# Hybrid gMLP and dilated-attention block on eight cores: V groups as separate keys, banks chosen by disuse, and a written-out order for the input part

## The reference

```
h = rms_norm(x, norm_mix_pre);  z = h @ w_in
u_a, v_a, q, k, v_b, g_a, g_b = split(z)
y_a = gelu(u_a) * (tril(w_s) @ layer_norm(gelu(v_a)) + b_s)   # in chunks of 128
y_b = mixture over (window, dilation) = (128,1), (512,4), (2048,16)
      of softmax attention with ALiBi, 16 heads of 64
merged = sigmoid(g_a + b0) * (y_a @ w_a_proj) + sigmoid(g_b + b1) * (y_b @ w_b_proj)
x = x + rms_norm(merged @ w_out, norm_mix_post)
out = x + rms_norm(square(relu(rms_norm(x, norm_ffn_pre) @ w_ff1)) @ w_ff2, norm_ffn_post)
```

## Time and profile before

| what | us |
|---|---|
| median of 3 runs (1236.28 to 1341.39) | 1237.54 |
| the profiled execution's own time | 1236.43 |
| its span, first to last instruction, core 6 | 1234.9 |
| spans of the 8 cores | 1231.5 to 1234.9 |
| first scores of pair 0 start | 59.99 |
| last V product of pair 7 | about 396 |

### The profile page before, as it was taken

How to read it: one execution, slowest core, us unless ns; L and a number is a source line. 1 busy time by engine, 2 the same in 40 slices (tenths; PEclk the granted TensorE clock), 3 DMA queues, 4 the chain that set the end, 5 groups by cost and what they waited for, 6 DMA issues and landing times.

```text
span 1234.9 us, 23134 instructions; the slowest of 8 cores (1231.5 to 1234.9 us)
## 1 busy us (share of the span) xinstructions
PE 1183.3 (96%) x8072; PEld 606.6 (49%) x8203; DVE 564.8 (46%) x971; ACT 544.3 (44%) x910; POOL 152.6 (12%) x207
## 2 busy tenths in 40 slices
PE   6899999999999999999999999999999999999997
PEld 3455655565566445544444444444444444444443
DVE  3656766676677867723223354400560046103303
ACT  4565776666687553221212464420552055204411
POOL 2100000000010547621100000000000101010100
PEclk8999999999999999999999999999999999999999
DMA  9521532431134579499972223625363536353741
GB/s 241 133 49 40 107 55 44 81 70 37 30 62 83 103 105 136 86 178 135 128 107 35 89 82 107 234 72 202 120 226 132 204 120 199 117 193 135 245 152 69
DMA packets 37106, 146.39 MB, mean 119 GB/s; under 512 B 5120, under 2 KB 5376, under 8 KB 28288
## 3 DMA queue, kind: packets, MB, share of 16 engines
q0 software_dynamic: 21504, 104.87, 37.4%
q1 hardware_dynamic: 15488, 40.03, 10.7%
HBM read 165.85 MB, written 25.17 MB: 155 GB/s over the span
## 4 chain that ended last, share of the span: by engine, by line
PE 87%; DVE 5%; issue 3%; ACT 2%; DMA 2%; DVEq 0%; SPq 0%; ACTq 0%; POOLq 0%
PE pss L259 36%; PE psc L259 27%; PE psa L259 21%; PE psa L353 2%; DVE sb_PT L519 2%; ACT sb_Et L498 1%; DMA sb_xt<-x 1%; DMA sb_wqkv<-w_qkv 1%; DVE sb_vaug L362 1%; DVE sb_VT L339 0%; DVE sb_bst L621 0%; DVE sb_ybT L568 0%; ACT sb_junk L288 0%; DVE sb_acc L559 0%; PE pss L304 0%
## 5 line engine op out<-in xcount | busy, mean ns | idle before, releaser
L498 ACT ACTIVATE sb_Et<-pss 128x1024 bf16<-128x1024 f32 x144 | 139.7, 1015 | 50.8 <-PE pss L259 34.8
L976 DVE TENSOR_TENSOR sb_hT<-sb_hT 128x512 bf16<-128x512 bf16 x128 | 50.8, 421 | 231.9 <-ACT sb_hT L974 231.9
L259 PE MATMUL psa<-sb_hT,sb_wqkv 128*128 128x512 bf16 x516 | 125.1, 382 | 12.7 <-DVE sb_vaug L362 3.8
L519 DVE TENSOR_TENSOR sb_PT<-sb_Et,sb_EBh 128x512 bf16<-128x512 bf16 x208 | 84.8, 422 | 24.8 <-ACT sb_Et L498 12.9
L764 ACT ACTIVATE sb_sg<-pss,sb_bg 128x512 f32<-128x512 f32 x50 | 34.4, 687 | 137.2 <-PE pss L259 126.3
L259 PE MATMUL pss<-sb_hT,sb_wg 128*128 128x512 bf16 x407 | 93.9, 379 | 0.5
L259 PE MATMUL pss<-sb_w2b,sb_hT 128*128 128x512 bf16 x283 | 84.6, 379 | 0.3
L777 DVE SCALAR_TENSOR_TENSOR sb_sg<-sb_sg,psc 128x512 f32<-128x512 f32 x50 | 34.4, 688 | 109.4 <-PE psc L259 109.4
L259 PEld LDWEIGHTS psa<-sb_hT,sb_wqkv 128*128 128x128 bf16 x552 | 49.3, 98 | 64.8 <-issue 14.3
L259 PE MATMUL pss<-sb_h2T,sb_w1b 128*128 128x512 bf16 x342 | 78.7, 379 | 0.5
L259 PE MATMUL psc<-sb_PT,sb_vaug 128*128 128x128 bf16 (+1 forms) x752 | 67.9, 232 | 0.4 <-DVE sb_PT L519 0.3
(11 more groups left out here) (201 smaller groups left out, 1938.9 us busy)
## 6 DMA issues: line engine op xcount, KB each, us to landing
sb_w1b<-w_bf POOLq DMA_DIRECT2D x23, 1024.0 KB, 6.9
sb_mgw<-w_bf POOLq DMA_DIRECT2D x21, 1024.0 KB, 7.1
sb_w2b<-w_bf POOLq DMA_DIRECT2D x18, 1024.0 KB, 6.6
w_bf<-w POOLq DMA_DIRECT2D x16, 1024.0 KB, 15.4
sb_xt<-x SPq DMA_DIRECT2D x16, 512.0 KB, 11.6
sb_denbc<-sb_lden SPq DMA_DIRECT2D x64, 128.0 KB, 2.3
sb_xo<-x SPq DMA_DIRECT2D x16, 512.0 KB, 6.2
sb_wqkv<-w_qkv POOLq DMA_DIRECT2D x24, 256.0 KB, 6.6
```

Of the source, the lines that this page charges most:

```text
L259: S.op("pe", lambda e: e.matmul(out, lhsT=lhsT, rhs=rhs, start=start, stop=stop, skip_group_check=True), reads=reads, writes=writes, signa ...
L498: S.op("act", lambda en: en.activation(out=e[:], in_=pS[:], func=AF.Exp), reads=[], writes=sk + [ek])
L519: S.op("dve", lambda en, h=h, eb2=eb2: en.tensor_tensor(out=v3(pt)[:, h, :].rearrange("p (a q) -> p a q", q=256), in0=v3(e)[:, h, :].rearr ...
L976: S.op("dve", lambda e, fb=fb: e.tensor_tensor(out=hid[:, fb, :], in0=hid[:, fb, :], in1=hid[:, fb, :], op=ALU.mult), reads=[], writes=[f" ...
```

## The change

1. **V groups.** Key `vaug{d}` becomes six keys `vaug{d}_0` to `vaug{d}_5`, one for each group; a copy writes its own and a PV reads the one that it needs.
2. **Order of the groups.** The six transposes of a pair now stand at 0.5, 1.5, 2.5, 3.5, 5.5 and 7.5, in the order (pattern, half) = (0,0), (2,0), (2,1), (1,0), (1,1), (0,1).
3. **Banks.** `fbank` gives the bank that was used longest ago, among 0 and 1, or among 0, 1, 6 and 7 for fills from 1.5 to 4.
4. **Input part.** A string lists the order of S, R, N, T, H (copy to `hT`), P (projection) and C (its copy). The copies of tiles 13 and 14 go to ACT. The first 8 loads of x are issued at once, tile 1 ahead of the gain row, and a load for tile i + 8 follows N of tile i. Weights wait for tiles 1 (K), 3 (Q) and 5 (V) instead of 2 (K), 4 (V) and 5 (Q). Warm matmuls: 24, 4, 12 instead of 24, 5, 5, 5.
5. **V2 and V3** move into pair 0's fill, behind the first scores; the loads for pair 2 follow them.

```diff
+    VA = [[f"vaug{i}_{c}" for c in range(6)] for i in range(2)]
...
+        if i in (13, 14):
+            S.op("act", lambda e: e.activation(out=o, in_=pv, func=AF.Copy), reads=[], writes=[PK[pk], f"hT{i}"])
...
+    used = {0: 0, 1: 0, 6: 0, 7: 0}
 
     def fbank():
+        pk = min((0, 1, 6, 7) if head[0] else (0, 1), key=lambda b: used[b])
         pctr[0] += 1
-        return (0, 6, 1, 7)[pctr[0] % 4] if head[0] else pctr[0] % 2
+        used[pk] = pctr[0]
+        return pk
...
-            S.op("dve", lambda e: e.tensor_copy(out=o, in_=i), reads=[], writes=[PK[pk], f"vaug{d}"])
+            S.op("dve", lambda e: e.tensor_copy(out=o, in_=i), reads=[], writes=[PK[pk], VA[d][2 * p + half]])
...
+    order = """S0 R0 S1 N0 R1 T0 S2 N1 H0 T1 S3 H1 R3 N2 S4 N3 T2 S5 H2 T3 H3 R5 PK0 N4 S6 N5 T4 CK0 PQ0 S7 H4 R7 T5 CQ0 N6 PV0
...
+    p1_load(0)
+    p1_load(1)
+    load("sp", gbc[:], gains_d[0:1, :].partition_broadcast(128), "gbc")
+    for i in range(2, 8):
+        p1_load(i)
+    for j, i in ((1, 1), (0, 3), (2, 5)):
+        wload(0, [f"xt{i}"], (j,))
     warm(24)
...
-            head[0] = 1.5 <= fill[0][0] < 5
+            head[0] = 1.5 <= fill[0][0] <= 4
...
-        fill = [(k, lambda p=i // 2, h=i % 2, hp=hp: vtr(hp, p, h)) for i, k in enumerate((0.5, 1.5, 2.5, 3.5, 4.5, 5.5))]
+        fill = [(k, lambda p=p, h=h, hp=hp: vtr(hp, p, h))
+                for k, p, h in ((0.5, 0, 0), (1.5, 2, 0), (2.5, 2, 1), (3.5, 1, 0), (5.5, 1, 1), (7.5, 0, 1))]
...
+        if hp == 0:
+            fill += [(w - 4, lambda w=w: proj(0, 2, w)) for w in (2, 3)]
...
-                           [f"vaug{d}", f"PTs{r // 4}"], [ack], False)
+                           [VA[d][(32 + r) // 8], f"PTs{r // 4}"], [ack], False)
...
-                       [f"vaug{d}", J["ptk"]], [ack], i == np_ - 1)
+                       [VA[d][(16 * J["p"] + kb) // 8], J["ptk"]], [ack], i == np_ - 1)
```

More of the change, by code:

```diff
@@ L279, in build_nc, with p1_load, p1_rs, p1_nrm @@
     load("sp", ident[:], ident_d[:, :], "ident")
+    VA = [[f"vaug{i}_{c}" for c in range(6)] for i in range(2)]
     for i in range(2):
-        S.op("pool", lambda e, i=i: e.memset(vaug[i][:, :, 64:128], 1.0), reads=[], writes=[f"vaug{i}"])
+        S.op("pool", lambda e, i=i: e.memset(vaug[i][:, :, 64:128], 1.0), reads=[], writes=VA[i])
+    def p1_load(i):
+        load("sp", xt[i % 8][:], x_d[128 * i:128 * i + 128, :], f"xt{i % 8}")
     def p1_sq(i):
         b = i % 8
-        load("sp", xt[b][:], x_d[128 * i:128 * i + 128, :], f"xt{b}")
-        if i == 0:
-            load("sp", gbc[:], gains_d[0:1, :].partition_broadcast(128), "gbc")
         S.op("act", lambda e: e.activation(out=junk[:], in_=xt[b][:], func=AF.Square, scale=1.0 / 32, accum_out=rstd[:, i:i + 1]),
              reads=[f"xt{b}"], writes=["junk", f"rstd{i}"])
-    def p1_nrm(tiles):
+    def p1_rs(tiles):
         rsq(rstd[:, tiles[0]:tiles[-1] + 1], EPS, [f"rstd{i}" for i in tiles])
[L293 to L297, removed]
+    def p1_nrm(i):
+        b = i % 8
+        S.op("dve", lambda e: e.scalar_tensor_tensor(out=xn[b][:], in0=xt[b][:], scalar=rstd[:, i:i + 1],
+                                                     in1=gbc[:], op0=ALU.mult, op1=ALU.mult),
+             reads=[f"xt{b}", f"rstd{i}", "gbc"], writes=[f"xn{b}"])
+        if i < 8:
+            p1_load(i + 8)
     def p1_tr(i):
@@ L359, in vtr @@
         if hp == 7 and half == 0:
-            S.op("act", lambda e: e.activation(out=o, in_=i, func=AF.Copy), reads=[], writes=[PK[pk], f"vaug{d}"])
+            S.op("act", lambda e: e.activation(out=o, in_=i, func=AF.Copy), reads=[], writes=[PK[pk], VA[d][2 * p + half]])
         else:
-            S.op("dve", lambda e: e.tensor_copy(out=o, in_=i), reads=[], writes=[PK[pk], f"vaug{d}"])
+            S.op("dve", lambda e: e.tensor_copy(out=o, in_=i), reads=[], writes=[PK[pk], VA[d][2 * p + half]])
     def vraw(n, hf):
@@ L370, in vraw @@
              reads=[], writes=[PK[pk], f"vr{n}"])
-    todo, later, copies = [], [], {}
-    groups = {0: [0], 1: [1], 14: [14], 15: [15]}
-    groups.update({i: [i - 1, i] for i in range(3, 14, 2)})
+    order = """S0 R0 S1 N0 R1 T0 S2 N1 H0 T1 S3 H1 R3 N2 S4 N3 T2 S5 H2 T3 H3 R5 PK0 N4 S6 N5 T4 CK0 PQ0 S7 H4 R7 T5 CQ0 N6 PV0
+        S8 H5 T6 S9 N7 CV0 H6 T7 R9 H7 S10 N8 PK1 N9 S11 T8 PQ1 H8 CK1 R11 S12 N10 T9 PV1 CQ1 H9 S13 N11 T10 CV1 H10 T11 R13
+        H11 S14 N12 PK2 R14 N13 S15 T12 PQ2 H12 CK2 N14 R15 T13 CQ2 N15 T14 H13 T15 H14 H15 PK3 PQ3 CK3 CQ3""".split()
     def warm(n):
@@ L378, in warm @@
             mm(ps[7], ident[:], ident[:].unsqueeze(1).broadcast_to([128, 4, 128]), True, True, ["ident"], [PK[7]], False)
-    warm(24)
[L381 to L406, removed]
+    p1_load(0)
[5 more added lines that the diff above has]
+        wload(0, [f"xt{i}"], (j,))
+    warm(24)
+    copies = {}
+    for o in order:
+        k, r = o[0], o[1:]
+        if k == "S":
+            p1_sq(int(r))
+        elif k == "R":
+            i = int(r)
+            p1_rs([i] if i < 2 or i > 13 else [i - 1, i])
+        elif k == "N":
+            p1_nrm(int(r))
+        elif k == "T":
+            p1_tr(int(r))
+            warm({0: 4, 1: 12}.get(int(r), 0))
+        elif k == "H":
+            p1_cp(int(r))
+        elif k == "P":
+            later = []
+            proj(0, "QKV".index(r[0]), int(r[1]), later)
+            copies[r] = later[0]
+        else:
+            copies.pop(r)()
+    wload(1, ["xt7"])
+    pctr[0] = 0
     for i in range(2):
@@ L474, in build_nc @@
             load("sp", bg[:], bg_d[:, :], "bg")
-        if hp < 6:
+        if hp == 0:
+            fill.insert(2, (-0.5, lambda: wload(2)))
+        elif hp < 6:
             wload(hp + 2)
@@ L573, in build_nc @@
             if hp == 7 and k == 1:
[L574 to L575 removed]
+                S.alias([f"vr{i}" for i in range(4)], VA[0])
+                S.alias([f"wua{i}" for i in range(8)], VA[0] + ["QT0", "KT0"] + [f"wqkv0{j}" for j in range(3)])
                 for i in range(8):
```

11 lines of the change are left out of this document (7 added, 4 removed).

## The result

The changed kernel took 1219.01 us (median of 4 runs, 1217.84 to 1219.88) beside 1236.28 us for the kernel before on the same chip: a ratio of 0.986, 95% interval 0.984 to 0.9879. That is 17.3 us, or 1.4%, less; the forecast was 1218.3, from 1213 to 1226.

A forecast was written before the change was run, and what follows sets the result against it. PE, busy 1183 of 1235 us, bounds the kernel, so only its standstills could pay: attention 16.2 plus input part 3.0 makes 19.2 us, from 1237.5 to 1218.3 us, range 1213 to 1226.

The forecast's parts named there:

- attention: Attention, all pairs: ended waits of PE for V copies and for banks give 16.2 us.
- the input part: Before pair 0: earlier K weights and a new order bring V2 and V3's end from 59.99 to 57.0, 3.0 us gained.
- The PV waits: First PV of each pair: waits for the copy of transposed V go, 7.84 us plus 1.40 in pair 7, 9.24 together.
- The banks: Attention's fill: bank of longest disuse ends projection waits (3.76), transpose waits (2.67) and 0.53 in pair 7, 6.96 us.
- Attention's bound: Attention: gain at least 9.2 us if bank choice only moves waits, at most 16.7 with pair 7's small rest.
- the next to be late: Attention, once cover is used up: scores' exponentials on ACT, or PV's own scores on DVE; no size given.
- lost cover: Ahead of pair 0's scores: PE idles 0.9 us for Q3's copy, which V3 covered before.
- Rival A: Input part gives nothing because V's weights land 1.6 us late: 1221.3 us, chance 0.20.
- B: Attention: only half of PE's waits go, since first PV still waits on DVE or bank waits move: 1226.4 us, chance 0.09.
- C: Input part runs as its engines allow and K1 comes early, 6 to 9 us gained there: 1213.5 us, chance 0.08.
- D: Slower: a pair's second transposes wait for banks 6 and 7 while the previous pair's sums are read: 1240 us, chance 0.03.
- The half-rate stretch at K2: Input part: K2's 7 matmuls took 2.98 us for 1.67 at clock 0.50; expected gone, or the same once.

The follow-up runs named there:

- the five old executions: Kernel before, and it with only the group keys and places, only the banks, only the keys, only the places: 1236.28, 1220.92, 1231.2, 1230.59, 1239.35 us.
- the three new ones: The kernel before with only the new input part (1235.46 us), and the changed kernel twice (1219.01 and 1219.38 us).
- The runs with later requests: Changed kernel with weights requested after tiles 2, 4, 5 instead of 1, 3, 5: 1217.78 us; the same with V2, V3 back in the input part: 1216.83 us.

## Why the prediction was right, and what in it was not

The total, 19.2 us for 17.3 measured, and the sign held. The two terms missed in opposite directions: attention gave 17.1 for 16.2, the input part 0.6 to 1.4 at the first transposes for 3.0, and no difference that the time shows in the run with it alone. That the time came within 0.7 of the 1218.3 is in part luck: the misses partly cancel, and the 1237.5 that the forecast starts from is 1.2 above the 1236.3 measured beside the result.

**The PV waits** (9.24): right, and shown by the waits of the changed kernel, where none is left, and by the two halves: the keys alone end a part of these waits, the places alone add to them.

**The banks** (6.96): right in size alone (6.78), wrong in what they add. The 3.76 us of the projections' waits end with the new places as well, so the step that gave them to the banks named one of two sufficient causes. For the sum this made no difference, since each wait was counted once.

**Attention's bound** ("at most 16.7"): exceeded by 0.4. On the profiled cores the first transposes came 2.04 us closer together from pair 0 to 1 (2.06 forecast), and 255.8 - 241.9 = 13.9 us closer from pair 1 to 7, where the sum had 12.2. Two waits of 0.3 that I had left out went as well:

```profile
PE psc L259 <- DVE sb_acc L559: 0.6, 2, 0.3
```

This row of the kernel before has no counterpart after. The other 1.0 us lies in gaps too short to have rows of their own, and I can't name it. Pair 7 gave 35.2 - 34.0 = 1.2 instead of 1.9. There PE now waits for the exponential of the scores, which I had called the next to be late:

```profile
350.46 0.41 PE L259 MATMUL pss<-sb_QT,sb_KT 64*128 64x128 bf16 x8 [0.30 <-ACT sb_Et L523]
```

**The input part** (3.0) is the step that failed. Its early part came as walked on the profiled core, V0 at 30.30 for 30.6 and K1 at 34.17 for 34.1, but not by the road that I took. K's weights landed at 18.6 instead of 22.1, and K0 then waited for the copy of tile 3; the request for V went out at 21.41, where I had taken over the load of Q before with its request at 19.13, and landed in 8.8 us instead of 11.4. That these two misses cancel is luck. K2 came at 42.90 for 42.0. I had given DVE 0.3 us of waiting in that window; it had 1.1, all of it ahead of copies of transposes (DVE's timeline of the changed kernel):

```profile
36.61 0.69 DVE L319 COPY sb_hT<-pss 128x1024 bf16<-128x1024 bf16 x1 [0.20 <-PE pss L308]
...
39.22 0.69 DVE L319 COPY sb_hT<-pss 128x1024 bf16<-128x1024 bf16 x1 [0.62 <-PE pss L308]
...
41.96 0.69 DVE L319 COPY sb_hT<-pss 128x1024 bf16<-128x1024 bf16 x1 [0.26 <-PE pss L308]
```

The largest, 0.62, is at the copy of tile 9, whose transposes stand behind Q1 on PE. One reading of the walk is off without touching the sum: a tile's transposes hold PE for 0.44 us from start to start (35.90 to 36.34 in the changed kernel); 0.66 is the length of their row. The scores came at 54.62 for 53.6, and the same 1.0 us is missing at the end: 62.87 to 60.96 at the first transposes of the profiled cores, 1.9 gained. The rest of the miss is the core: I walked core 6 of one execution, the latest of its eight (59.99 against a median of 57.93 at the first scores), and set an expected walk against it. Over all cores the gain is 1.4 us between these two executions and 0.6 between the middle ones of all that have either input part. Counted from K1 to the first transposes, the 26.8 us of the changed kernel lie 0.7 below the 27.5 of an old core with the half-rate stretch at K2, such as core 6, and 0.7 above the 26.0 of one without. So from K1 on the change gains only where that stretch goes, and loses elsewhere; the rest is K1's own start, whose median over the cores lies between 33.2 and 34.1 in the five old executions and between 32.5 and 33.7 in the three new ones.

I had taken V2 and V3 behind the scores as work that only changes places, less 0.9 us of lost cover. The runs with them put back show 2.1 us from K1 on: two covers were lost, ahead of the scores and ahead of K3.

**Rival A** (the input part gives nothing) was nearer to the input part than the forecast, and its cause is partly there: the request for V goes out about 1 us later in the median of the cores when K's weights are asked for early, where A had 1.6. But V0 started at 30.30 and not after 32, which was to show A. The Trainium skill, "DMA: Bandwidth & Descriptors", section "Queues, rings and completion order", has each DMA engine serve the queues with work in turn; the trace agrees with that direction. The runs with later requests show that it decides nothing here: their request for V goes out earlier, but its weights land no earlier. **B** is excluded by the waits, **C** by the windows (8.73 and 7.22, not 7.6 each from an early K1), **D** by the start of pair 1, where 1.5 us was left between the sums' copies and the second transposes.

**The half-rate stretch at K2**: right; in the changed kernel no core shows one after 35 us, while 7 of 8 cores before had one of 3.4 us between 41 and 48. The number varies: in the four other executions with the old input part 2, 3, 3 and 5 of the 8 cores show one behind K1.

## What to carry to other kernels

A dependence key for a whole buffer makes each reader wait for the youngest writer, so finer keys and an order that puts the needed pieces first belong together: here 4.5 us for the keys, 3.2 lost by the order, 13.6 gained by both. When several causes can end one wait, do one part alone before booking it. Before moving work from a phase that waits into one that doesn't, list the waits that this work covers, and compare phases over all cores, not on the latest one, from a point behind which the cores agree (here K1).
